# Split products for two more row groups of an output projection, their remainders on GpSimd, and a reordered end

## The reference, cut to what matters

```python
# first block, in each of its two layers
mix = concatenate([y_conf, y_sb, y_ret, y_sc], axis=-1) @ w_out[l]   # 256x1024 @ 1024x1024
x = x + rms_norm(mix, norm_mix_post[l])
f = conv_ffn(rms_norm(x, norm_ffn_pre[l]), ...)
...
# second block: a token mixer, then 32 experts (4 per token), then
return rmsnorm(x, final_norm_g)
```

## Time and profile before

| | |
|---|---|
| median of three executions | 2049.01 us |
| the profiled execution | 2049.59 us |
| its span | 2047.8 us |
| around the span | 1.8 us |
| PE busy | 1938.0 us, 95% |
| DVE busy | 915.7 us, 45% |
| ACT busy | 644.4 us, 31% |
| POOL busy | 10.6 us, 1% |
| read from HBM | 587.54 MB |

### The profile page before, as it was taken

How to read it: one execution, slowest core, us unless ns; L and a number is a source line. 1 busy time by engine, 2 the same in 40 slices (tenths; PEclk the granted TensorE clock), 3 DMA queues, 4 the chain that set the end, 5 groups by cost and what they waited for, 6 DMA issues and landing times.

```text
span 2047.8 us, 26788 instructions
## 1 busy us (share of the span) xinstructions
PE 1938.0 (95%) x11046; PEld 1281.3 (63%) x11046; DVE 915.7 (45%) x1565; ACT 644.4 (31%) x1086; POOL 10.6 (1%) x24
## 2 busy tenths in 40 slices
PE   8999999999998999999999999999999989899888
PEld 8979998979996677877898333333333333333332
DVE  6877677977766337456656211111111111111112
ACT  5565556565556324355644100000000000000001
POOL 0000000010000000000000000000000000000000
PEclk9999999999999999999999999999999999999999
DMA  8345544445546644031448999999999999999997
GB/s 316 118 165 199 185 165 168 153 180 207 185 165 267 244 172 171 32 122 43 157 176 356 372 421 433 433 432 431 430 431 432 433 432 433 430 431 431 432 432 309
DMA packets 45164, 589.90 MB, mean 288 GB/s; under 512 B 5328, under 2 KB 6032, under 8 KB 10960
## 3 DMA queue, kind: packets, MB, share of 16 engines
q1 hardware_dynamic: 43296, 583.09, 69.7%
q0 software_dynamic: 1488, 5.28, 0.9%
q10 hardware_dynamic: 288, 0.24, 0.0%
HBM read 587.54 MB, written 1.05 MB: 287 GB/s over the span
## 4 chain that ended last, share of the span: by engine, by line
PE 73%; DMA 20%; DVE 3%; ACT 3%; issue 1%; SPq 0%; DVEq 0%; ACTq 0%
PE psum L2113 46%; PE psum L2589 19%; DMA slots<-exp_w_dram 11%; DMA work<-exp_w_dram 7%; PE psum L2534 3%; PE psum L2715 3%; DVE split_weights L1635 0%; DMA slots<-ada_w_dram 0%; DVE work L1461 0%; ACT work L959 0%; ACT split_rows L988 0%; ACT split_weights L1145 0%; DVE work L1779 0%; PE psum L2133 0%; PE psum L2260 0%
## 5 line engine op out<-in xcount | busy, mean ns | idle before, releaser
L2589 PE MATMUL psum<-slots,work 128*64 128x512 f32 x2304 | 516.4, 600 | 52.4 <-DMA slots<-exp_w_dram 44.2
L2113 PE MATMUL psum<-split_rows,split_weights 128*128 128x256 f32 (+1 forms) x3792 | 506.3, 295 | 6.4 <-DVE split_rows L1402 3.4
L2113 PEld LDWEIGHTS psum<-split_rows,split_weights 128*128 128x128 f32 x3792 | 483.9, 192 | 31.0 <-issue 11.0
L2589 PEld LDWEIGHTS psum<-slots,work 128*64 128x64 f32 x2304 | 166.8, 138 | 364.8 <-issue 329.6
L1423 DVE TENSOR_TENSOR split_weights<-slots,split_weights 128x1024 fp32r<-128x1024 f32 x180 | 219.5, 1223 | 121.3 <-ACT split_weights L1003 120.4
L1003 ACT ACTIVATE split_weights<-slots 128x1024 fp32r<-128x1024 f32 x180 | 190.4, 1062 | 184.8 <-PE psum L2113 164.8
L2113 PE MATMUL psum<-split_weights,split_rows 128*128 128x512 f32 x1008 | 233.5, 391 | 0.0
L2113 PEld LDWEIGHTS psum<-split_weights,split_rows 128*128 128x128 f32 x1008 | 188.3, 188 | 41.9 <-issue 3.3
L2078 DVE TENSOR_SCALAR work<-psum 128x512 f32<-128x512 f32 x32 | 22.0, 687 | 388.3 <-PE psum L2589 388.3
L2589 PE MATMUL psum<-work 128*64 128x512 f32 x768 | 173.0, 603 | 17.1 <-DMA work<-exp_w_dram 17.1
L1331 ACT ACTIVATE work<-work 128x512 f32<-128x512 f32 x32 | 20.2, 631 | 475.4 <-DVE work L2078 475.4
(11 more groups left out here) (284 smaller groups left out, 1360.4 us busy)
## 6 DMA issues: line engine op xcount, KB each, us to landing
slots<-exp_w_dram SPq DMA_DIRECT2D x68, 4096.0 KB, 29.8
work<-exp_w_dram SPq DMA_DIRECT2D x23, 4096.0 KB, 29.8
slots<-w_in_dram SPq DMA_DIRECT2D x56, 1024.0 KB, 6.0
slots<-ffn_up_dram SPq DMA_DIRECT2D x44, 1024.0 KB, 4.8
slots<-ada_w_dram SPq DMA_DIRECT2D x24, 1024.0 KB, 8.6
slots<-ffn_down_dram SPq DMA_DIRECT2D x20, 1024.0 KB, 4.8
slots<-w_out_dram SPq DMA_DIRECT2D x12, 1024.0 KB, 4.8
slots<-exp_w_dram SPq DMA_DIRECT2D x4, 2048.0 KB, 8.6
```

The costliest lines, as they stand in the source:

```text
L2113: return nc.tensor.matmul(out_, lhsT, rhs, start=first, stop=last)
L2589: return nc.tensor.matmul(b[rows, :], lhs[:, rows], rhs, start=first, stop=last, skip_group_check=True)
```

## The change

- SB's two row groups become split products. ACT writes their high parts into two free buffers of split weight units before it evacuates SB0 and SB1; it evacuates those banks as high parts, into the space of `catT` that lay around the SB columns, and DVE subtracts for the low parts, between its last convolution tap and the short convolution. PE runs 12 split products where it ran a `tokens_down` over one group.
- All six low parts of w_out's split groups are made by GpSimd, in the order of need, from `out_high` and the new high parts. DVE's `out_low` is gone.
- In each pair of experts ACT evacuates the turned activations AT2 right behind sigmoid 0 instead of behind sigmoid 1 and ST.
- The final norm: ACT squares each bank as soon as it is summed and writes the squares to a scratch tile; DVE multiplies each bank by the gain when it has been squared, and scales by the inverse root afterwards, in place.

```diff
@@ tiles
+        sb_units = [split_w[:, WEIGHTS_AT + 2 * i * UNIT:WEIGHTS_AT + 2 * (i + 1) * UNIT].rearrange("p (s n) -> p s n", s=2) for i in (0, 1)]
+        sb_split = split_work[:, CAT_AT + 2 * T:CAT_AT + 6 * T].rearrange("p (s k t) -> p s k t", s=2, k=2)
...
+        def sb_rows(i):
+
+            return half_place(13 % RING)[:, i * UNIT:(i + 1) * UNIT]
@@ gpsimd
+            for l in range(DEPTH):
+                for i in (0, 1):
+                    pool.wait_ge(sb_units_high, 2 * l + i + 1)
+                    nc.gpsimd.tensor_tensor(sb_units[i][:, 1, :], sb_rows(i), sb_units[i][:, 0, :], ALU.subtract
+                                            ).then_inc(sb_units_split, 1)
+                for i in range(4):
+                    pool.wait_ge(out_high_ready, 4 * l + i + 1)
+                    nc.gpsimd.tensor_tensor(out_split[i][:, 1, :], out_rows(i), out_split[i][:, 0, :], ALU.subtract
+                                            ).then_inc(out_split_ready, 1)
@@ scalar, layer
+                take(act, ("s", 11), l)
+                half_ready(act, 13, l)
+                for i in (0, 1):
+                    nc.scalar.activation(sb_units[i][:, 0, :], sb_rows(i), ACT.Copy).then_inc(sb_units_high, 1)
                 for c in (0, 1):
-                    evac(("SB", c), l, catT[:, 2 + c, :], take(act, ("SB", c), l)[:, 0:T])
+                    nc.scalar.activation(sb_split[:, 0, c, :], take(act, ("SB", c), l)[:, 0:T], ACT.Copy).then_inc(sb_high_ready, 1)
@@ scalar, pair
+                        if n == 0:
+                            evac(("AT2", 0), it, flat(actT[:, 0:4, :]), take(act, ("AT2", 0), it))
                     evac(("ST", 0), it, spread_T, take(act, ("ST", 0), it)[:, 0:T])
-                    evac(("AT2", 0), it, flat(actT[:, 0:4, :]), take(act, ("AT2", 0), it))
@@ scalar, final norm
-                        act.wait_ge(combined, 3 * PAIRS * n + (1 + t if half else 0))
+                        if half + t == 0:
+                            act.wait_ge(expert_slot_free, 6 * PAIRS * n + 4)
+                        else:
+                            act.wait_ge(combined, 3 * PAIRS * n + (1 + t if half else 0))
                         i = 2 * t + half
-                        step(nc.scalar.activation(xhat[:, t, 512 * half:512 * half + 512], psum[:, i, :], ACT.Square,
-                                                  accum_out=half_sumsq[:, i:i + 1]), l)
+                        nc.scalar.activation(act_[t], psum[:, i, :], ACT.Square, accum_out=half_sumsq[:, i:i + 1]
+                                             ).then_inc(last_squared, 1)
+                        act.wait_ge(last_squared, 2 * half + t + 1)
@@ vector, layer
                 conf_taps(26, CONF_K)
+                for c in (0, 1):
+                    dve.wait_ge(sb_high_ready, 2 * l + c + 1)
+                    nc.vector.tensor_tensor(sb_split[:, 1, c, :], take(dve, ("SB", c), l)[:, 0:T], sb_split[:, 0, c, :], ALU.subtract
+                                            ).then_inc(evacuated[bank_of(("SB", c))], 1)
...
-                out_low(0)
...
-                out_low(1)
@@ vector, final norm
-                dve.wait_ge(combined, 3 * PAIRS * n + 2)
-                for t in range(TT):
+                def gained(t, half):
+
+                    cut = slice(512 * half, 512 * half + 512)
+                    dve.wait_ge(last_squared, 2 * half + t + 1)
+                    step(nc.vector.tensor_tensor(xhat[:, t, cut], psum[:, 2 * t + half, :], final_row[:, cut], ALU.mult), L2)
+
+                def scaled(t):
+
                     inverse_rms(8 * L2 + t + 5, t)
                     for half in (0, 1):
                         cut = slice(512 * half, 512 * half + 512)
-                        nc.vector.scalar_tensor_tensor(out=xhat[:, t, cut], in0=psum[:, 2 * t + half, :],
-                                                       scalar=rinv[:, t:t + 1], in1=final_row[:, cut],
-                                                       op0=ALU.mult, op1=ALU.mult).then_inc(out_ready, 1)
+                        nc.vector.tensor_scalar(xhat[:, t, cut], xhat[:, t, cut], rinv[:, t:t + 1], None, ALU.mult
+                                                ).then_inc(out_ready, 1)
+
+                gained(0, 0)
+                gained(1, 0)
+                gained(0, 1)
+                scaled(0)
+                gained(1, 1)
+                scaled(1)
@@ tensor, layer
-                tokens_down("M", l, 6, catT, (2,), True, False, None)
+                def sb_products(i):
+
+                    pe.wait_ge(sb_units_split, 2 * l + i + 1)
+                    for b in range(4):
+                        t, half = divmod(b, 2)
+                        for p_, (a, v) in enumerate(PASSES):
+                            mm(psum[:, bank_of(("M", b)), :], sb_split[:, v, i, t * P:(t + 1) * P],
+                               sb_units[i][:, a, half * 512:half * 512 + 512], i + p_ == 0, False)
+
+                sb_products(0)
                 pe.wait_ge(conf_sq_ready, l + 1)
...
-                tokens_down("M", l, 6, catT, (3,), False, False, None)
+                sb_products(1)
```

More of the change, by code:

```diff
@@ L587, in build_program @@
         out_high_ready, out_split_ready = sem("w_out_high_ready"), sem("w_out_split_ready")
+        sb_units_high, sb_units_split, sb_high_ready = sem("sb_units_high"), sem("sb_units_split"), sem("sb_high_ready")
         cat_high_ready, cat_split_ready = sem("cat_high_ready"), sem("cat_split_ready")
+        last_squared = sem("last_half_rows_squared")
         third_part_loaded = sem("third_slot_part_loaded")
@@ L1550, in layer @@
                 nc.vector.tensor_reduce(ret_var, sqg, AX, ALU.add).then_inc(ret_var_ready, 1)
[L1551 to L1556, removed]
                 after_evacuation(dve, ("CV", 0), l)
```

## The result

The changed kernel takes 2069.0 us (median of four runs, 2065.29 to 2073.06) against 2049.45 us for the kernel before (four runs, 2048.88 to 2050.86): a ratio of 1.0091 with a 95% interval of [1.0079, 1.0103]. That is 19.6 us slower. The forecast of no change was wrong, its range ended 0.5 us too low, and what came is the size of rival A, 2068.1. The profiled execution is the longest of the four, 2073.06 us; its span is 2071.3.

A forecast was written before the change was run, and what follows sets the result against it. PE bounds up to about 1,300 us, then the expert weights set the pace. 2049.59 + 0.1 - 0.8 = 2048.9, and with the median 0.58 lower 2048.3, the same time (chance 0.50); range 2045.7 to 2068.5.

The forecast's parts named there:

- rival A: At the last taps, GpSimd's SBUF-reading subtractions block DVE instructions with two SBUF inputs: +19.8 us, 2068.1; chance 0.32.
- the paragraph on GpSimd: Output projection: six subtractions at 2.48 us meet PE's due times, cost nothing; at the upper bound +1.1 us a layer.
- Rival B: Output projection: POOL waits for DVE or is slow by itself, about +5.5 us a layer, 2059; chance 0.12.
- Rival C: Variance not late (-3.0), DMA idle won back (-2.6), norm gives 0.8: 2042.6; chance 0.06.
- the saved PE work: SB groups as split products: 7.09 us removed, 5.58 added, PE's work falls by 1.51 us a layer.
- PE and DVE around the variance: Two low halves (0.75 us) delay the squares, PE waits 1.2 us, nothing of 1.51 is left: +0.05 us a layer.
- ACT's two high halves: Ahead of SB's evacuation: 1.00 us each, inside 2.34 us of ACT idle; cost nothing.
- DVE's four remainders taken out: Output projection: 2 x 2.35 us off DVE gives nothing, since PE does not wait for DVE at 425.52.
- Pairs of experts: ACT turns AT2 around before the second sigmoid and spread matrix: taken as 0, bound a gain of 2.6 us.
- Final norm: At the end: squares start on the first bank, 0.9 us sooner; last output 2043.6 against 2044.40, gain 0.8 us.

The follow-up runs named there:

- experiment 2: The changed kernel with all six remainders given back to DVE and POOL left idle: 2052.96 us, ratio 1.0011 to the kernel before.
- experiment 3: The changed kernel with each GpSimd subtraction replaced by a memset of the same tile, writing but reading nothing: 2050.60 us, ratio 1.0003 to the kernel before.
- experiment 4: The changed kernel with GpSimd's first subtraction of a layer waiting for the last convolution tap: 2068.58 us, ratio 1.0091 to the kernel before.
- experiment 6: The kernel before with only its four remainders moved from DVE to GpSimd: 2055.92 us, ratio 1.0018 to the kernel before.
- experiment 1: The kernel before with only the new ACT order in the pairs and the new final norm: 2049.28 us against 2050.10, ratio 1.0001.
- experiment 7: The changed kernel with 12 more thrown-away products on PE ahead of its wait for the last tap: 2066.30 us, ratio 1.0067 to the kernel before.
- experiment 5: The changed kernel with each GpSimd subtraction cut into two of 512 columns: profiled execution 2063.57 us, a second 3938.35 us, no ratio.
- experiment 8: The changed kernel with each GpSimd subtraction replaced by a copy that reads one tile: 2054.20 us, ratio 1.0018 to the kernel before.

## Why the prediction was wrong, point by point

**The failed step** is in the paragraph on GpSimd: "With nothing in its way POOL begins at 406.14 + 1.0 = 407.1", and behind the due times, "Cost nothing". The price of a subtraction was right: 2.48 us taken, 2.44 and 2.57 measured. (Half of the Trainium skill's figure for 2048 columns, in GPSIMD Engine Reference, Elementwise — side-by-side cycle accounting, is 2.25 us, an estimate; the trace has 9 to 14% more.) Its start was right too: 1.67 us after the first of the ten taps where 1.6 was forecast. Its place off the critical path was wrong. The list of due times asked only when PE needs each unit, and each was in time. It didn't ask which DVE instructions stand under POOL's 10 us. They are the last taps, which PE waits for next, so the cost is not nothing but 8.38 us a layer. Experiments 2, 3 and 4 show it from three sides: take the subtractions or their reads away from POOL and the taps are back at 4.04 us, move them and the hold moves with them.

**The evidence was read too weakly.** Against rival A the prediction set L1402, which runs unheld beside a GpSimd DMA. But L1402 reads one bank and one SBUF tile, and such an instruction isn't held even beside a subtraction: L1541 in experiment 6 keeps its 0.74 us for two. So that row was evidence on neither side. Nor was the row for it, the DMA issue of 0.85 us beside L1374: L1374 reads one tile and a column of statistics, not two tiles, and its twelve instances in the kernel before all take 0.75 to 0.76 us. The next issue moves something else, and no profile has the one of 0.85 us alone, so its length doesn't show whether there was a hold. What was left was the rule of the Trainium skill (SBUF — State Buffer, Who interferes with whom). By that rule, the trace agrees: held are the taps and L1584 (two SBUF inputs), not held are the reduction and the reciprocal (one input), and a POOL that only writes holds nothing, 4.04 us in experiment 3. The chance of 0.32 was small for a mechanism with a stated rule for it and no row against it.

**Rival A's own sum** was 4 x 2.48 = 9.9 us a layer; 8.38 was measured, because each turn lets one tap of 0.40 through, which is tap time that had to be spent anyway (4 x (2.5 - 0.4) = 8.4). Over two layers that is 3.0 us less, and 2.5 came back as something that no case had: the clock of PE behind a wait of 8.85 us, +0.9 and +1.6. So the total fits partly by luck: against the 2049.01 of before A's 2068.1 is +19.1; +18.0 is accounted for, 19.6 lies between the medians.

**Rival B** named a real thing, POOL waiting for DVE, but in the changed kernel POOL is held little (2.3 to 2.6 us each); experiment 6 shows it, 3.28 for the first. Its 431.5 doesn't follow from the terms it gives: 412.0, 2.5 for the second unit, 9.9 and 3.5 make 427.9. **Rival C** fell with experiment 3: even without any hold the variance waits 0.93 us for ACT, so the saved PE work isn't won.

**PE and DVE around the variance.** Forecast: two low halves at 0.75 us, a wait of about 1.2 us before the variance, and +0.05 us a layer in sum. Measured without the hold (experiment 3): 0.74, 0.93, and -0.16. Right within about 0.3 us. The variance came 4.82 us after the column sums where 5.15 was forecast, mostly because it followed the squares by 0.05 us (412.91, 412.96): the 0.30 us that the forecast kept between them was PE's own work in the earlier trace rows. Against that, 12 split products took 3.03 and 3.10 us where 2.79 was forecast.

**ACT's two high halves** took 1.99 us in ACT's idle, its evacuations behind them still waited 0.45 us for PE, as rows of experiment 2 and of the changed kernel have it. Nothing, as forecast. **DVE's four remainders taken out:** the fp32 list of the kernel before ends without a wait of PE for DVE, so nothing was to be won, as forecast.

**Pairs of experts:** forecast 0, and experiment 1 as a whole is 1.0001. Right within 2 us. **Final norm:** forecast -0.8, measured -0.70. The first bank's square starts early as drawn; the two scalings took 0.88 us instead of the 0.75 borrowed from L1374.

## What to carry to other kernels

Before giving work to GpSimd, list the DVE instructions that will run under it and mark those with two SBUF inputs and each TENSOR_SCALAR. If such an instruction is on the chain, count for each GpSimd instruction that reads SBUF its own duration less one DVE instruction. Here moving the four subtractions left 8.0 us a layer of that cost, and cutting each in two left 7.5, of 8.4. A list of due times that are all met shows that the consumer isn't late; it doesn't show that the helper disturbs nobody. And a saving on the bounding engine is worth only what the second chain leaves: here 1.51 us of PE work by the forecast came to 0.16 us, because the low halves made the squares 0.75 us later and the squares had 0.30 us to spare.

## What the runs showed of the hardware that was not expected

- A TENSOR_SCALAR with a single SBUF tensor as input is held as well: 2.20 us each in experiment 4 (4.40 for two) instead of 0.30, and 0.94 instead of 0.17 in experiment 6 (L1550, 128x8). The Trainium skill (SBUF — State Buffer, Who interferes with whom) has this operation among those that can enter a two-port mode and then contend; the trace agrees. The prediction had expected this only of instructions with two such inputs. The reciprocal on a tile of the same 128x256 isn't held (1.74 us beside POOL, 1.75 in the kernel before).
- The two engines take turns one instruction at a time while both have work ready: POOL's four subtractions started 2.5 us apart with one tap between each two. In experiment 6 two taps of the short convolution in a row started and ran unheld after POOL's first subtraction had started, which took 0.95 us longer than the later ones, so the order isn't a strict alternation. What decides it was not tried.
- After 8.85 us without work, PE ran at or near the 1.2 GHz level from 427 to 433 us (granted clock 0.50 and 0.55) and was at 1.00 behind. Kept busy with 8.01 us of products (experiment 7), it stayed at 1.00. Shorter waits did it too: behind 7.29 us (experiment 4) the clock was 0.50 from 432 to 436 us, behind 5.53 us (experiment 5) 0.50 from 420.6 to 426, where the first 12 split products took 5.10 us, and behind 2.81 us (experiment 8) 0.68 from 414 to 418, where they took 3.98. Such a wait costs more than its length.
